# Step-zero column transposes and split rate computation in a two-layer hybrid trunk

## The reference

```
z = xn @ w_in                                  # one projection for all branches
y_a = rglru_branch(...)                        # per-channel recurrence
y_b = gdn_branch(...)                          # chunked gated delta rule, 8 heads of 128
y_c = rwkv7_branch(...)                        # 16 heads of 64
merged = g_a*(y_a @ p_lru) + g_b*(y_b @ p_gdn) + g_c*(y_c @ p_rwkv)

# rglru_branch: the rates
log_a = (-LRU_C * r) * softplus(-lam)          # softplus(-lam) is one number per channel

# chunked_gated_delta_rule, chunks of 64 tokens
g = cumsum(g)                                  # decays, per head and token
decay = exp(where(incl, g[:, None] - g[None, :], -inf))
k_beta = k * beta[..., None]
a_mat = where(strict, (k_beta @ k.T) * decay, 0)
rhs = concat([v * beta, k_beta * exp(g)])      # solved against I + a_mat
q_dec = q * exp(g);  k_dec = k * exp(g[-1] - g)
# q and k are first l2-normalised: x * rsqrt(sum(x*x) + 1e-6)
```

## Time and profile before

| | |
|---|---|
| median of 3 runs | 3174.31 us (3172.84 to 3175.81) |
| profiled execution, its own time | 3171.77 us |
| its span in the profile | 3170.0 us |
| TensorE busy | 3109.4 us (98%) |
| VectorE busy | 2240.5 us (71%) |
| ScalarE busy | 1726.1 us (54%) |
| mean granted TensorE clock | 0.997 |

### The profile page before, as it was taken

One profiled execution on the slowest core, in us unless ns is written; L12 is line 12 of the kernel. 1 busy time (PEld: TensorE's weight loads), 2 busy tenths in 40 slices (PEclk: granted clock), 3 DMA queues, 4 the chain that ended last, 5 costly groups with the idle time before them and its releaser, 6 DMA issues. The chain is left out here.

```text
span 3170.0 us, 73251 instructions
## 1 busy us (share of the span) xinstructions
PE 3109.4 (98%) x24672; PEld 2752.3 (87%) x24672; DVE 2240.5 (71%) x4909; ACT 1726.1 (54%) x3666; POOL 280.0 (9%) x270
## 2 busy tenths in 40 slices
PE   8999999999999999999999999999999999999998
PEld 7999889889897888888889998898899978888887
DVE  6777576667886677777776775766588767777776
ACT  6665554442595555555565665443426855555555
POOL 1323111110000000000022321112000000000000
PEclk9999999999999999999999999999999999999999
DMA  4332232233225555555542322322422265555554
GB/s 171 103 103 89 75 121 93 93 123 131 96 70 182 190 186 191 192 185 188 177 153 86 109 76 91 118 93 93 173 90 85 73 199 186 186 195 188 186 189 162
DMA packets 122815, 434.95 MB, mean 137 GB/s; under 512 B 15808, under 2 KB 18112, under 8 KB 122048
## 3 DMA queue, kind: packets, MB, share of 16 engines
q1 hardware_dynamic: 122688, 433.31, 39.7%
HBM read 432.21 MB, written 1.05 MB: 137 GB/s over the span
## 5 line engine op out<-in xcount | busy, mean ns | idle before, releaser
L2618 PE MATMUL bank<-x_both,u_parts 128*128 128x512 f32 x1536 | 557.8, 397 | 1.7 <-DVE u_parts L2728 1.7
L2602 PE MATMUL bank<-v_parts,act_high 128*128 128x512 f32 x1024 | 405.3, 396 | 1.8 <-issue 1.5
L2728 DVE TENSOR_TENSOR u_parts<-u_raw,u_parts 128x512 fp32r<-128x512 f32 x384 | 265.7, 692 | 191.2 <-ACT u_parts L2671 191.2
L2604 PE MATMUL bank<-v_parts,act_low 128*128 128x512 f32 x1024 | 399.8, 390 | 0.0
L2614 PE MATMUL bank<-x_both,u_parts 128*128 128x256 f32 x1536 | 399.5, 281 | 0.0
L2603 PE MATMUL bank<-v_parts,act_high 128*128 128x512 f32 x1024 | 398.8, 389 | 0.0
L354 PE MATMUL bank<-x_parts,w_parts 128*128 128x256 f32 x1248 | 388.7, 311 | 3.4 <-DVE w_parts L339 2.0
L2558 DVE TENSOR_TENSOR v_parts<-v_raw,v_parts 128x512 fp32r<-128x512 f32 x512 | 330.1, 686 | 33.7 <-ACT v_parts L2553 32.1
L355 PE MATMUL bank<-x_parts,w_parts 128*128 128x256 f32 x1248 | 352.6, 283 | 0.0
L356 PE MATMUL bank<-x_parts,w_parts 128*128 128x256 f32 x1248 | 352.2, 282 | 0.0
L2671 ACT ACTIVATE u_parts<-u_raw 128x512 fp32r<-128x512 f32 x384 | 242.5, 632 | 187.7 <-PE bank L2618 147.3
(11 more groups left out here) (385 smaller groups left out, 6216.7 us busy)
## 6 DMA issues: line engine op xcount, KB each, us to landing
v_raw<-in_v SPq DMA_DIRECT2D x256, 512.0 KB, 3.5
u_raw<-in_u SPq DMA_DIRECT2D x192, 512.0 KB, 4.1
ring<-in_w_side SPq DMA_DIRECT2D x80, 512.0 KB, 3.6
ring<-in_w_gdn SPq DMA_DIRECT2D x64, 512.0 KB, 3.5
ring<-in_w_rwkv SPq DMA_DIRECT2D x46, 512.0 KB, 3.6
ring<-in_w_gdn_side SPq DMA_DIRECT2D x32, 512.0 KB, 3.5
ring<-in_u SPq DMA_DIRECT2D x32, 512.0 KB, 3.9
u_ring<-in_u SPq DMA_DIRECT2D x32, 512.0 KB, 3.5
```

What stands on the lines that cost most here:

```text
L2602: te.matmul(ps, f32r(w_hi), f32r(x_hi), start=start, stop=False, **kw)
L2604: return te.matmul(ps, f32r(w_lo), f32r(x_hi), start=False, stop=stop, **kw)
L2618: mm = te.matmul(banks[r % 4][:, :].rearrange("p (x t) -> p x t", x=2), f32r(u_hi[:, cols]), f32r(x_both[:, :, k]), start=(k == 0), stop=( ...
L2728: v.tensor_tensor(f32r(u_lo[:, half(n)]), u_raw[:, r % 2, half(n)], u_hi[:, half(n)], ALU.subtract).then_inc(u_low, 1)
```

## The change

Decays, betas and norms are turned into rows by transposing the column itself, read 128 times with a step of zero (`to_broadcast`), so `GB` and `RB` and their VectorE copies are gone; the summed decay is taken from `st[:, 2]`, where it stood already. Side tile 1 is multiplied in two parts, its first two of eight k-tiles where the five filler matmuls stood, the other six behind `rsq`. The transposes of v stand ahead of the rows. ScalarE takes the Silu ahead of its wait for the round before, and `eg` and the scaled v ahead of the decays' Exp; VectorE makes `DT0` behind the scaled keys. The rates are split: nine instructions after the inverse's level 2, seven behind the first half of the tile `f0` at level 4.

```diff
@@ softplus_log is now three functions; softplus_log calls them in turn @@
+    def softplus_log_terms(v, V, z2, p, ks):
+        for k in ks:
             v.wait_ge(V.sem, V.now())
             v.scalar_tensor_tensor(p, p, 1.0 / (2 * k + 1), z2, ALU.add, ALU.mult).then_inc(V.sem, V.one())
@@ class Lru @@
+        def vector_rates_begin(self, v):
+            x, e, z, z2, p, m = self.small
             v.wait_ge(self.pload, 32)
             v.tensor_scalar(self.small[0], self.par[:, :, self.c["lam"]], -1.0, None, ALU.mult).then_inc(self.V.sem, self.V.one("neg"))
             v.wait_ge(self.S.sem, self.S.at("sp_e"))
             v.wait_ge(self.V.sem, self.V.now())
-            softplus_log(v, self.V, *self.small)
+            softplus_log_begin(v, self.V, e, z, z2, p)
+            softplus_log_terms(v, self.V, z2, p, range(7, 4, -1))
+
+        def vector_rates_end(self, v):
+            x, e, z, z2, p, m = self.small
+            softplus_log_terms(v, self.V, z2, p, range(4, 0, -1))
+            softplus_log_end(v, self.V, x, z, p, m)
             v.wait_ge(self.V.sem, self.V.now())
@@ rwkv vec_body @@
                     else:
                         W.skip(v, W.low, tile("r", NI), 3)
+                        lru.vector_rates_begin(v)
...
                 if n == 4:
                     vec_rest(v, i, "f0", (0,))
+                    if not more:
+                        lru.vector_rates_end(v)
...
-            if not more:
-                lru.vector_rates(v)
@@ gdn pe_side: takes the k-tiles, signals after the last @@
-            project(te, ps_g[n], 4 + n, (ya, yc)[n // 2]).then_inc(EG.sem, EG.one(f"g{n}"))
+            mm = project(te, ps_g[n], 4 + n, (ya, yc)[n // 2], ks)
+            if ks[-1] == KT - 1:
+                mm.then_inc(EG.sem, EG.one(f"g{n}"))
@@ gdn pe_body @@
             pe_side(te, i, 0, more)
-            turn(te, b6, 5)
+            pe_side(te, i, 1, more, range(0, 2))
...
-            for x, (bk, m) in enumerate(((b4, upto), (b5, ident))):
-                for q in range(4):
-                    mm = te.matmul(four(bk)[:, q], GB[:, x, q], m, start=True, stop=True)
-                mm.then_inc(E.sem, E.one(("gcrow", "brow")[x]))
             for q in range(4):
                 mm = te.transpose(four(b7)[:, q], Z[:, 4 + q // 2, (q % 2) * P:(q % 2 + 1) * P], ident)
             mm.then_inc(E.sem, E.one("vT"))
+            for x, bk in enumerate((b4, b5)):
+                for q in range(4):
+                    mm = te.transpose(four(bk)[:, q], st[:, (2, 1)[x], q:q + 1].to_broadcast([P, P]), ident)
+                mm.then_inc(E.sem, E.one(("gcrow", "brow")[x]))
 
             te.wait_ge(V.sem, V.at("RB", i))
             for x, bk in enumerate((b2, b3)):
                 for q in range(4):
-                    mm = te.matmul(four(bk)[:, q], RB[:, (4, 0)[x] + q], ident, start=True, stop=True)
+                    mm = te.transpose(four(bk)[:, q], rs[:, (4, 0)[x] + q:(4, 0)[x] + q + 1].to_broadcast([P, P]), ident)
                 mm.then_inc(E.sem, E.one(("rsk", "rsq")[x]))
-            pe_side(te, i, 1, more)
+            pe_side(te, i, 1, more, range(2, KT))
@@ gdn act_body @@
+            a.activation(Z[:, 0:6], Z[:, 0:6], ACT.Silu).then_inc(S.sem, S.one("silu"))
             a.wait_ge(V.sem, V.before("y", i))
-            a.activation(Z[:, 0:6], Z[:, 0:6], ACT.Silu).then_inc(S.sem, S.one("silu"))
...
+            a.wait_ge(E.sem, E.at("gcrow", i))
+            a.activation(eg, four(b4), ACT.Exp).then_inc(S.sem, S.one("eg"))
+            for q in range(4):
+                a.activation(Vt[:, q], four(b7)[:, q], ACT.Copy, scale=st[:, 1, q:q + 1]).then_inc(S.sem, S.one("Vt"))
             a.wait_ge(V.sem, V.at("DT0", i))
             a.activation(DT, DT, ACT.Exp).then_inc(S.sem, S.one("DT"))
@@ gdn vec_body @@
-            v.tensor_copy(GB, st[:, 0:2].unsqueeze(3).to_broadcast([P, 2, 4, P])).then_inc(V.sem, V.one("GB"))
...
-            v.reciprocal(rs, rs).then_inc(V.sem, V.one())
-            v.wait_ge(V.sem, V.now(i))
-            v.tensor_copy(RB, rs.unsqueeze(2).to_broadcast([P, 8, P])).then_inc(V.sem, V.one("RB"))
-            v.wait_ge(E.sem, E.at("gcrow", i))
-            for q in range(4):
-                v.tensor_scalar(DT[:, q], four(b4)[:, q], st[:, 2, q:q + 1], 0.0, ALU.subtract, ALU.min)\
-                    .then_inc(V.sem, V.one("DT0"))
+            v.reciprocal(rs, rs).then_inc(V.sem, V.one("RB"))
...
             v.tensor_tensor(KQ[:, :, 0], KN, four(b5), ALU.mult).then_inc(V.sem, V.one("kb"))
+            v.wait_ge(S.sem, S.at("eg", i))
+            for q in range(4):
+                v.tensor_scalar(DT[:, q], four(b4)[:, q], st[:, 2, q:q + 1], 0.0, ALU.subtract, ALU.min)\
+                    .then_inc(V.sem, V.one("DT0"))
```

More of the change, by code:

```diff
@@ L372, in softplus_exp, with softplus_log_begin @@
         a.activation(e, e, ACT.Exp, scale=-1.0).then_inc(S.sem, S.one(tag + "_e"))
-    def softplus_log(v, V, x, e, z, z2, p, m):
+    def softplus_log_begin(v, V, e, z, z2, p):
         v.tensor_scalar(z, e, 2.0, None, ALU.add).then_inc(V.sem, V.one())
@@ L385, in softplus_log, with softplus_log_end @@
         v.tensor_scalar(p, z2, 1.0 / 17, None, ALU.mult).then_inc(V.sem, V.one())
-        for k in range(7, 0, -1):
+    def softplus_log_terms(v, V, z2, p, ks):
+        for k in ks:
             v.wait_ge(V.sem, V.now())
             v.scalar_tensor_tensor(p, p, 1.0 / (2 * k + 1), z2, ALU.add, ALU.mult).then_inc(V.sem, V.one())
+    def softplus_log_end(v, V, x, z, p, m):
         v.wait_ge(V.sem, V.now())
@@ L393, in softplus_log @@
         v.scalar_tensor_tensor(p, p, 2.0, m, ALU.mult, ALU.add).then_inc(V.sem, V.one())
+    def softplus_log(v, V, x, e, z, z2, p, m):
+        softplus_log_begin(v, V, e, z, z2, p)
+        softplus_log_terms(v, V, z2, p, range(7, 0, -1))
+        softplus_log_end(v, V, x, z, p, m)
     class Lru:
@@ L437, in scalar_rates @@
             softplus_exp(a, self.S, self.par[:, :, self.c["lam"]], self.small[1], "sp")
-        def vector_rates(self, v):
+        def vector_rates_begin(self, v):
+            x, e, z, z2, p, m = self.small
             v.wait_ge(self.pload, 32)
@@ L1575, in vec_rest, with pe_side @@
             W.rest(v, ring[:, s % 4], 8 * i + s, s % 2)
-        def pe_side(te, i, n, more):
+        def pe_side(te, i, n, more, ks=range(KT)):
             te.wait_ge(loaded_g[n], 16 * i + 16)
@@ L1786, in act_body @@
             a.activation(rs, rs, ACT.Sqrt).then_inc(S.sem, S.one("rs"))
+            a.wait_ge(E.sem, E.at("gcrow", i))
+            a.activation(eg, four(b4), ACT.Exp).then_inc(S.sem, S.one("eg"))
+            for q in range(4):
+                a.activation(Vt[:, q], four(b7)[:, q], ACT.Copy, scale=st[:, 1, q:q + 1]).then_inc(S.sem, S.one("Vt"))
             a.wait_ge(V.sem, V.at("DT0", i))
             a.activation(DT, DT, ACT.Exp).then_inc(S.sem, S.one("DT"))
-            a.activation(eg, four(b4), ACT.Exp).then_inc(S.sem, S.one("eg"))
-            a.wait_ge(E.sem, E.at("vT", i))
-            for q in range(4):
-                a.activation(Vt[:, q], four(b7)[:, q], ACT.Copy, scale=st[:, 1, q:q + 1]).then_inc(S.sem, S.one("Vt"))
             a.wait_ge(E.sem, E.at("kT", i))
```

## The result

The changed kernel takes **3134.41 us** (median of 4 runs, 3131.0 to 3139.46), where before took 3174.55 (3172.84 to 3175.81): ratio 0.9878, 95% interval 0.9865 to 0.989. The prediction was 3139.7 with 3132 to 3156.

The account below looks back on a forecast made before the run. TensorE, busy 98% of the span, was taken as the bound. Savings of 25.6 us in the delta net rounds and 10.4 for the rates, less 1.4 for the logarithms, gave 34.6 us: 3139.7 us, range 3132 to 3156.

Parts of the forecast that it names:

- Filler: In each delta net round, removing TensorE's filler matmuls saves 1.11 us; the two k-tiles replacing them are only moved.
- Decays, betas and norms: In each delta net round, transposes at 0.11 us replace products at 0.23: 1.0 us saved on decays and betas, 0.93 on norms.
- the step-zero load as dear as a product: Rival: 128 step-zero transposes take 0.23 us instead of 0.11, 15 us come back, 3155; chance 0.10.
- the slow one: Rival: a weight load reading one address 128 times is slow in itself; 3190 at 0.5 us a transpose; chance 0.03.
- The price of the copy `RB`: On VectorE ahead of the norms: keeping this 0.69 us copy would make TensorE wait 0.4 us.
- The last round of a layer: In each layer's last delta net round, covering a 0.59 us wait and longer filler raises the saving to 3.8 us.
- T0: Behind side tile 2, TensorE needs `TT0`: 0.1 to 0.3 us of slack left, no wait; otherwise up to 0.3 a round.
- the logarithms: Behind the last RWKV round's first state, they wait for GpSimd on the shared port: 0.7 us a layer, 1.4 lost.
- The rates, 10.4 us: In the last RWKV rounds, the first state starts 3.4 us earlier in each layer, plus 3.6 from the clock: 10.4 us.
- The clock behind the rates: In the last RWKV rounds, the clock's fall behind the removed wait goes too: 2.56 and 1.02 us back.
- The other fall, at 1970: A 3.4 us fall of the clock at 1970 with TensorE busy; its going, 1.7 us, was allowed in the range.
- The rival of the clock in the delta net rounds: Rival: transposes replacing full matmuls make the clock fall, 1.7 us each; 3146 for half the rounds, 3153 for all; chance 0.14.

Follow-up runs that it names:

- run 10: The changed kernel with side tile 1 in one piece behind the norms' transposes and no filler: 3140.92 us, ratio 0.9891.
- run 5: The changed kernel with the filler turn back and side tile 1 in one piece: 3150.8 us, ratio 0.9923.
- run 3: The changed kernel with the sixteen step-zero transposes of a round made as full matmuls of the same columns with the identity: 3153.08 us, ratio 0.9923.
- run 7: The changed kernel with VectorE spreading columns into `GB` and `RB` again, the transposes reading these contiguous columns: 3140.12 us, ratio 0.9891.
- Runs 4: The changed kernel with `DT0` ahead of the norms on VectorE and its Exp first on ScalarE, as before: 3136.78 us, ratio 0.9873.
- run 8: The changed kernel with GpSimd's masks in two parts, levels 2 to 5 only behind VectorE's products for the state: 3132.01 us, ratio 0.9866.
- run 1: The changed kernel with the rates whole again in their old place, ahead of the last RWKV round's first state: 3143.0 us, ratio 0.9898.
- run 2: The kernel before with only the rates split in two parts: 3164.44 us, ratio 0.9962.
- run 6: The changed kernel with the logarithms one step later in the last RWKV round, away from GpSimd: 3135.01 us, ratio 0.9874.
- run 11: The changed kernel with GpSimd's masks split in a layer's first three rounds and the opening's narrow products divided around the first projection: 3130.93 us, ratio 0.986.
- run 12: The changed kernel with only the opening reordered: 8 narrow products, the first projection, the other 8: 3132.99 us, ratio 0.9866.
- run 9: The changed kernel with GpSimd's masks in two parts in the first three rounds of a layer only: 3133.82 us, ratio 0.9868.

## Why the prediction held, step by step

**Filler, 1.11 us a round.** Right. Side tile 0 to side tile 2 is 13.09 us, and run 10 against run 5 isolates it. That the two k-tiles of side tile 1 would only be moved is right for TensorE (run 10: 13.10) and wrong for the round, see below.

**Decays, betas and norms, 1.93 us a round.** Right, 1.81 by run 3. The choice of 0.11 us for an operation that no row showed was the large bet of the sum. Run 7 settles it: contiguous or step zero, 0.109 us. Two rivals fall with it, the step-zero load as dear as a product and the slow one. The price of the copy `RB`, argued from `0.99 us behind the start of L1648`, was 0.4 us; run 7 has 0.40.

**The last round of a layer, 3.8 us.** Right: the interval of ss into the last round shrank by 4.22 us (64.44 to 60.22), of which 3.48 are what every round gives, so its own extra is 0.74 against 0.8 forecast.

**T0.** Right: 0.34 us of slack, and in no round a wait.

**Behind T0: the term that was left out.** The sum took everything behind T0 as unchanged. It became shorter, by 0.45 us in a round and 0.3 in the last: 1.65 a layer, 3.3 in all, the largest error of the sum. In the rounds, 2.7 of the 3.3, it is this: VectorE splits weights there while GpSimd masks, and the pair takes 1.29, 1.88 or 2.35 us by how they meet. Runs 4, 5 and 10 start GpSimd's masks 0.3 us earlier against T0, each by another edit, and each brings back 2.34 or 2.35 for the pair and 33.86 to 33.88 for the way to U0; run 8 brings 1.29 by parting them. The 0.3 of the last round, 0.6 in all, is something else: no pair stands there, the masks take about 8.95 us before and after, and runs 4 and 10, with the masks started early again, keep 16.25. Its cause stays open. The Trainium skill, "SBUF — State Buffer", section on the two separate sides, has the two engines' shared port pair as an exclusive lock for a whole instruction, whichever starts first. The trace agrees: GpSimd's ten masks take 9.33 us where VectorE's pair takes 2.33, and 9.68 where it takes 1.88, so most of what one gains the other pays. I used that rule in the prediction for the logarithms, and did not look for other places where both engines work.

**The rates, 10.4 us less 1.4 for the logarithms.** Measured 10.05 by the trace (5.79 and 4.26), 8.6 by run 1, 11.3 by run 2. The wait is gone to the last tenth: state at 373.02, its bank's product begun at 372.60. The logarithms wait as I said (2.13 us for 0.86 of work), and the second state comes 0.66 us late (3.86 against 3.20 in run 6), which is the 0.7 of the sum. But the third follows 2.76 us later instead of 3.20, so 0.44 of it comes back, and by run 6 the round's end moves only 0.03. I priced a late state as a late round, though VectorE waits for TensorE ahead of each undisturbed state (1.53 and 0.75 us in run 6).

**The clock behind the rates.** Right, and more firmly than by one trace. In before and run 1, rates in the old place, the clock fell 13 to 17 us ahead of the last yT in 4 layers of 4; in the twelve profiles of the new place in 0 of 24. The wait brings the fall; at the old place it costs about 1.0 us where it lasts 3.4.

**The other fall, at 1970.** I took it as possible either way, and it is: it was gone in the changed kernel's profile, but not by the change as far as the other profiles tell. It is worth 1.7 us: from the last yT to the first ss the kernel before took 39.33 us in the first layer and 41.01 in the second. A fall 4.8 to 6.9 us behind the last yT, where the narrow products end, stands in 12 of the 24 layers of all kernels up to run 10, in kernels with transposes and with products alike; the two of run 11 and the two of run 12 have none. With four layers against a chance of one half, that is not proof (one in sixteen). Nor is the narrowed spread, since the times of run 6, of run 7 and of run 9 each lie within 2.7 us too, with a fall in the profile. The clock has a part in the changed kernel's median being 3.4 us above its profiled run: the runs of 3131.0 and 3131.72 have a mean clock of 0.999, those of 3137.11 and 3139.46 have 0.998. Two such falls would be 3.4 us; the slowest run is 8.5 above the profiled one, and it was not traced.

**The rival of the clock in the delta net rounds** had no part in it. The sums and twenty transposes in a row (487.08 to 491.00), 3.9 us, brought no fall in the rounds of the changed kernel. The rival's fear was not empty, though: in the 88 rounds of the eleven kernels with transposes the clock fell once (run 10, at 1987.61), amid such a row and at a cost of 1.7 us. In the 24 rounds of the three kernels with products it fell twice, both in run 2.

The sum: 34.6 forecast, 40.8 measured between the profiled runs. Of the 6.2 between them 2.7 are VectorE's pair behind T0, 0.6 the last rounds behind T0, 1.7 the clock at 1970, 1.05 the logarithms and the rates (10.05 for 9.0), and 0.1 the rest.

The range held with some luck. The large errors lie on one side, and two of the four runs, the profiled one among them, came out below the 3132 at which the range began. The median is above it because the two others, whose mean clock was lower, took 3137.11 and 3139.46.

## What to carry to other kernels

Where TensorE is full, look for products that only copy or spread: a transpose of a column read with step zero makes the same rows at half the price, and the spread copy goes too, with the wait behind it. When a change moves the start of a GpSimd task by some tenths, read what VectorE does during all of that task, not only at its start; a pair of weight splits cost 1.88 or 2.35 us by that alone, and 1.29 where the masks left it free. And price a stall of a helper engine only by what it pushes beyond its next wait.

## What was not expected of the hardware

- A 128x128 f32 transpose takes 0.109 us start to start and one record, an f32 product of that shape 0.22 to 0.23 and two. Reading the transposed operand's column with step zero changes neither.
- A row of 16 products of 128x16 in 3.5 us, without idle time, was followed by a granted clock of 0.50 in 12 of 24 layers. The wait of 2.7 us in a chain of small products, in the RWKV round with the rates in the old place, was in 4 of 4. The sums and transposes of a delta net round were in 1 of 88.
- Three `tensor_scalar` operations with one SBUF input, 128x256 f32, are held by a GpSimd operation with two: 2.13 us instead of 0.86 (run 6).
